# Moving VectorE's softplus steps and an early read by a step in a two-block transformer kernel

## What is computed

```python
def first_block(x, c, ...):
    mod = silu(c) @ w_ada + b_ada                 # 6 x 2048 modulation values
    sh1, sc1, gt1, sh2, sc2, gt2 = split(mod, 6)
    h = rmsnorm(x, g_mix) * (1 + sc1) + sh1
    x = x + (1 + gt1) * mixer(h, ...)             # stick-breaking and sparse attention
    ...

def stick_breaking_attention(q, k, v):            # 8 heads of 128
    z = (q @ k.T) * scale
    log1m = where(past, -softplus(z), 0.0)
    after = cumsum(log1m, reverse=True) - log1m
    w = where(past, exp(log_sigmoid(z) + after), 0.0)
    return w @ v
```

## Time and profile before

| | before |
|---|---|
| median of 3 runs | 2651.7 us (2651.5 to 2653.85) |
| the profiled execution | 2650.92 us |
| its span in the trace | 2649.1 us |
| mean granted clock of TensorE | 0.989 |
| PE busy | 2598.1 us (98%) |
| DVE busy | 1876.9 us (71%) |
| ACT busy | 1236.9 us (47%) |

### The profile page before, as it was taken

The page is one execution under the profiler, slowest core; times in us unless marked ns, Lnnn a source line. Parts: engine busy times, 40 slices in busy tenths (PEclk is TensorE's granted clock), DMA queues, the critical chain, the costliest instruction groups (busy, mean ns, idle before and its releaser), DMA issues. The chain is left out here.

```text
span 2649.1 us, 40816 instructions
## 1 busy us (share of the span) xinstructions
PE 2598.1 (98%) x15329; PEld 2272.6 (86%) x15329; DVE 1876.9 (71%) x2659; ACT 1236.9 (47%) x1625; POOL 129.4 (5%) x203
## 2 busy tenths in 40 slices
PE   7999999999999999999999999999999999999998
PEld 4899888888888888888888888888888888888887
DVE  3468788887888888855666659999776645566554
ACT  3345544445645565544555541115544433444443
POOL 0021122001010000000000000000000000000000
PEclk8999999999999999999999999998999999999999
DMA  9997689768786877755665554554666655666654
GB/s 366 351 303 243 212 263 297 213 200 249 233 265 214 256 244 246 235 190 191 187 186 189 190 158 145 151 151 128 192 189 186 190 189 191 188 187 189 190 183 136
DMA packets 525077, 560.60 MB, mean 212 GB/s; under 512 B 20453, under 2 KB 487841, under 8 KB 524688
## 3 DMA queue, kind: packets, MB, share of 16 engines
q1 hardware_dynamic: 504448, 487.39, 58.3%
q0 software_dynamic: 20496, 71.38, 9.0%
HBM read 553.45 MB, written 2.10 MB: 210 GB/s over the span
## 5 line engine op out<-in xcount | busy, mean ns | idle before, releaser
L1121 DVE TENSOR_TENSOR wlo<-raw,whi 128x1024 fp32r<-128x1024 f32 x794 | 970.4, 1224 | 662.5 <-ACT whi L691 655.8
L691 ACT CAST whi<-raw 128x1024 fp32r<-128x1024 f32 x794 | 830.9, 1050 | 1042.4 <-PE ps L1939 910.9
L1937 PE MATMUL ps<-xhl,whi 128*128 128x512 f32 x3712 | 1172.1, 397 | 6.2 <-DVE wlo L1121 2.8
L1939 PEld LDWEIGHTS ps<-xhl,wlo 128*128 128x128 f32 x3712 | 699.0, 188 | 165.4
L1939 PE MATMUL ps<-xhl,wlo 128*128 128x256 f32 x3712 | 730.9, 278 | 0.0
L1937 PEld LDWEIGHTS ps<-xhl,whi 128*128 128x128 f32 x3712 | 566.8, 189 | 10.2 <-issue 5.6
L1937 PE MATMUL ps<-ghl,whi 128*128 128x512 f32 x1024 | 319.5, 393 | 0.0
L1939 PEld LDWEIGHTS ps<-ghl,wlo 128*128 128x128 f32 x1024 | 192.2, 188 | 44.5
L2297 PE MATMUL ps<-xg,raw 128*128 128x256 f32 x1024 | 221.5, 379 | 0.0
L1937 PE MATMUL ps<-fhl,whi 128*128 128x512 f32 x704 | 219.3, 392 | 0.0
L2297 PEld LDWEIGHTS ps<-xg,raw 128*128 128x128 f32 x1024 | 194.5, 190 | 26.4
(11 more groups left out here) (341 smaller groups left out, 1931.4 us busy)
## 6 DMA issues: line engine op xcount, KB each, us to landing
raw<-in_w_in SPq DMA_DIRECT2D x176, 512.0 KB, 4.9
raw<-in_w_up SPq DMA_DIRECT2D x176, 512.0 KB, 3.6
raw<-in_ffn_w_up SPq DMA_DIRECT2D x128, 512.0 KB, 3.8
raw<-in_ffn_w_down SPq DMA_DIRECT2D x128, 512.0 KB, 3.4
ada<-in_w_ada POOLq DMA_DIRECT2D x109, 512.0 KB, 5.0
raw<-in_w_down SPq DMA_DIRECT2D x88, 512.0 KB, 3.4
att<-in_w_ada SPq DMA_DIRECT2D x32, 1024.0 KB, 11.1
raw<-in_conv_w_pw SPq DMA_DIRECT2D x128, 256.0 KB, 3.3
```

What stands on the lines that cost most here:

```text
L691: nc.scalar.copy(whi[t % SPL][:, :, :], raw[t % RAW][:, :, :]).then_inc(s_hi, 1)
L1121: nc.vector.tensor_tensor(wlo[t % SPL][:, :, :], raw[t % RAW][:, :, :], whi[t % SPL][:, :, :].bitcast(F32), ALU.subtract).then_inc(s_lo, 1)
L1937: mm(o[:, m, :, :], whi[t % SPL][:, c, m * P:(m + 1) * P], x, start=first and c == 0, stop=last and c == KC - 1, skip_group_check=True)
L1939: ins = mm(o[:, m, 0, :], wlo[t % SPL][:, c, m * P:(m + 1) * P], x[:, 0, :], start=False, stop=last and c == KC - 1, skip_group_check=True)
```

## The change

Two places in VectorE's queue change. The read of the first columns of a pair stands behind unit `k = 3`'s split in place of `k = 4`'s. The four softplus steps of head `h` stand in step `25 + 2h` in place of `24 + 2h`: behind split `2s + 5`, two iterations later. The sum (L1387) stays in the even step. The queues of the other engines and all waits are as before.

```diff
@@ -1322,7 +1322,7 @@
                 j, k = t // 10, t % 10
                 c = 4 * (j + 1)
-                if k == 4:
+                if k == 3:
                     read_first(2 * j + 2)
                 if k == 5:
                     read_first(2 * j + 3)
@@ -1385,7 +1385,7 @@
                 if (s - B_STICK) % 2 == 0 and 1 <= h <= HEADS:
                     dve.wait_ge(s_af, h)
                     nc.vector.tensor_tensor(tD[:, :], tD[:, :], bank_f[:, 0:384], ALU.add).then_inc(s_w, 1)
-                if (s - B_STICK) % 2 == 0 and 0 <= h < HEADS:
+                if (s - B_STICK) % 2 == 1 and 0 <= h < HEADS:
 
                     dve.wait_ge(s_soft, h + 1)
                     sv.did(nc.vector.tensor_scalar(tB[:, 0:384], bank_z[:, 0:384], SCALE, 0.0, ALU.mult, ALU.max))
```

## The result

The changed kernel takes 2655.5 us (median of 22 runs, 2652.6 to 2658.3), the kernel before 2652.6 in as many runs of its own (2648.8 to 2655.2). The ratio is 1.0012, with a 95% interval of 1.0006 to 1.0017: +2.9 us, between 1.6 and 4.5. The profiled execution took 2656.2 us, 2654.4 of them span.

The account below looks back on a forecast made before the run. VectorE's waits for ScalarE were taken to hold up TensorE in the stick stage; -2.0 us (read) and +7.0 (later softplus) gave +5.0, between +3.6 and +8.4: 2656.7 us, range 2650.0 to 2660.5.

Parts of the forecast that it names:

- slower: Outcome above the border of 2657.0 us, 0.2% over the kernel before; chance 0.47.
- same: Outcome of no change that a measurement can tell, within about 0.2% (5.3 us); chance 0.41.
- Bound: Stick stage, 215 to 342 us: VectorE's busy time plus its waits sets the length; TensorE idles 6.0 us.
- The new wait of VectorE: Stick heads: the wait moves to the weight split (L1121), 4.67 us in place of 3.46; 6.5 us over all heads.
- TensorE's path: End of stick stage: last suffix sum 8.7 us later from the late softplus; waits of 1.5 to 4 us in nearly every head.
- What comes back: At 372 to 376 us: TensorE's waits of 2.13 and 0.70 us absorb delay, 8.4 - 2.8 = 5.6.
- The transfers' path: Near 372 us: landings released by VectorE's steps come 6.5 to 7.5 us late; the later path decides.
- the +7.0 of the sum: Cost in us at the end of moving the softplus steps one step later, range 5.6 to 8.4.
- The read: First modulation read, 66 to 105 us: waits of 1.63 and 0.35 us go; -2.0 us, range 0 to -2.0.
- The clock rival: Stick stage: TensorE's last new wait lowers its clock, nothing returns at 372 us; +8.1 us, 2659.8 us, chance 0.17.

Follow-up runs that it names:

- soft_by_one: The changed kernel with the softplus steps one iteration later than in the kernel before, instead of a step; 2653.2 us, ratio 1.0005.
- after_notable: The changed kernel with ScalarE's logarithm replaced by a second exponential, so that no table is loaded; 2645.2 us, ratio 0.9973.
- after_spread: The changed kernel with the exchanges of resident weights near 372 us spread over more steps; 2653.8 us, ratio 1.0010.
- before_spread: The kernel before with the exchanges of resident weights near 372 us spread over more steps; 2648.1 us, ratio 0.9987.
- read_only: The kernel before with only the read moved, softplus steps left in the even step; 2647.3 us, ratio 0.9980.
- soft_only: The kernel before with only the softplus steps moved one step later, the read left in place; 2659.3 us, ratio 1.0026.
- log_first_before: The kernel before with only ScalarE's softplus chain put ahead of the exponential that needs VectorE's sum; 2639.0 us, ratio 0.9946.

## Why the prediction was right, by its steps

**How near, and how much of it was luck.** The forecast was +5.0 us, and +2.9 came. That is below the +3.6 at which the sum's own bounds end, and +5.0 is outside the measured interval (1.6 to 4.5). The time of 2655.5 is 1.2 below 2656.7, and not 2.1, only because the kernel before took 2652.6 us in these runs and not the 2651.7 that the forecast was put on. The prediction also gave "slower" (0.47) a little more than "same" (0.41), and it is "same" that came. What it had right is the account of the loss; the gain was sized too small.

**Bound.** Right in the main. Most of what changed is idle time of TensorE, and in the stick stage VectorE's idle time set the length, as soft_by_one and after_notable show.

**The new wait of VectorE.** Right to 0.1 us. The distances between the sums of consecutive heads, after against before, and what was predicted for each:

| head | 1 | 2 | 3 | 4 | 5 | 6 | 7 |
|---|---|---|---|---|---|---|---|
| before, us | 14.97 | 15.82 | 16.35 | 15.30 | 16.23 | 16.35 | 14.70 |
| after, us | 15.04 | 16.44 | 17.54 | 15.91 | 16.84 | 17.57 | 15.91 |
| longer by | 0.07 | 0.62 | 1.19 | 0.61 | 0.61 | 1.22 | 1.21 |
| predicted | 0.1 | 0.6 | 1.21 | 0.6 | 0.6 | 1.21 | 1.21 |

With head 0 (3.6 - 5.53 + 2.85 = +0.9, predicted 1.0) edit 2 costs VectorE 6.5 us, as predicted. What made this possible is that a chain on one engine is a sum of rows: 1.80 us of the row behind the last sum and 2.87 us of the chain gave 4.67, and 4.66 came.

**TensorE's path.** Right in size: +8.7 us predicted for the last suffix sum from edit 2, 8.8 measured (6.0 + 2.8). The waits before the logits (L2117) came in heads 1 to 7, but four of the seven were below the 1.5 us that I had given as the least for nearly all, and one was above the 4 us (0.45, 1.36, 1.58, 3.55, 0.48, 1.36 and 4.53).

**What comes back.** 2.8 us were taken off TensorE's path at 372 us, and +5.6 became +2.7: right. after_spread and before_spread show that this is idle time filled up. The transfers' path, which I let decide and which made 5.6 into 7.0, did not decide in the kernel after: with the transfers spread it stands at 579.6 at the mark, without at 579.8. Edit 2 measured by itself is nevertheless about the +7.0 of the sum: 6.4 us at 577 us on top of the read (579.8 - 573.4) and 7.4 without it, of which 0.6 is that execution's; timed +6.9 alone and 8.2 on top of the read. That the +7.0 fits is in part luck, since the path that it was put on did not decide. The two edits meet in the same idle time near 372 us, so their shares can't be told apart to 1 us.

**The read.** This is the term that was mis-sized: -2.0 was taken, the end of its range. Timed it is -5.3 alone (2.9 to 7.7) and -4.0 beside edit 2 (+2.9 against +6.9). At the last column product it is -2.8 in the profiled executions of before and after, at 577 us -3.7 in that of read_only. Three things were missed.

First, the waits shown are not all that was lost. The first product starts 1.9 us earlier (66.79 to 64.86) where a wait of 1.63 was shown. From the first to the second product of the middle pair 9.03 us pass before and 8.78 after, though the trace of before has no wait there; soft_only shows one of 0.54 us. In the last pair it is 9.30 and 8.78, where 0.35 was shown. Second, the read gains 0.9 us more around 372 us, where TensorE waits less: from the last value product to the mark read_only takes 226.6 us, before 227.5. Third, the wait sometimes costs clock. Four executions had the wait of 1.6 to 1.8 us at 65 us, eight had not. With it the last group of column products started at 145.1, 145.7, 147.0 and 148.1; without it, at 142.4 to 143.0. The latest of the four, log_first_before, had a granted clock of 0.64 from 66 to 70 us, in its table of windows:

```profile
66.00:70.00 4.00, 3.18 (x16) 3.21 (x17) 3.10 (x7) 1.28 (x2) 0.00 (x0) 0.64 0.94 253
```

At this mark the read is thus worth 2.8 to 5.6 us, 3.9 on the average of these executions, and with it the sum would be -3.9 + 7.0 = +3.1. That is reckoned after the fact and from four executions only; how often the kernel before loses clock there isn't shown, and its profiled execution did not. I had weighed the clock against the change, behind new waits, and had not weighed it for the change, behind waits that go.

**The clock rival.** In the stage itself the clock is 0.97 before and after. Behind the wait of 4.53 us it is low. VectorE's head 7 is longer by 1.21 us all the same, just as predicted without the clock, so VectorE's pace wasn't touched, as argued:

```profile
326.00:330.00 4.00, 4.00 (x21) 3.91 (x20) 3.96 (x6) 0.00 (x0) 0.72 (x1) 0.58 0.92 256
```

Open is whether the 3 us near 650 us have more than chance to do with the change.

## What to carry to other kernels

Before moving work behind a wait, look at what the other engine does in its queue between the event and the release: an operation that needs a late result, placed ahead of independent ones, makes all of them late, and here moving the waiting side only renamed the wait. The chain of one head could be summed from rows to 0.1 us, so do this sum for both orders of both engines before choosing. A removed wait of TensorE can be worth more than its length (here 2.0 us shown and 2.8 to 5.6 measured), for the clock behind it is sometimes at the lower level. And look for idle time further down that will hide part of a loss today and not in the next version.

## What the runs showed of the hardware

The same wait of TensorE costs clock in one execution and not in another. At 65 us four executions waited 1.6 to 1.8 us; the granted clock from 66 to 70 us was 1.00, 1.00, 0.76 and 0.64, and the column products then ended up to 3 us apart. In the stick stage before waits 1.84 us and read_only 1.83 us at the same product (L2188), and behind it the clock was 0.65 in one and 1.00 in the other (before first, read_only second, from the tables of windows):

```profile
274.00:278.00 4.00, 3.88 (x22) 3.91 (x23) 3.96 (x5) 0.00 (x0) 0.66 (x1) 0.65 0.75 243
```

```profile
271.00:275.00 4.00, 3.68 (x31) 3.71 (x32) 3.96 (x6) 0.00 (x0) 0.72 (x1) 1.00 0.76 226
```

Near 650 us the kernel before waits 2.23 us and keeps 1.00, and the kernel after waits 1.96 us and has 0.83; read_only waits 2.34 us and has 0.83 too (before first, after second):

```profile
640.00:660.00 20.00, 17.77 (x105) 15.50 (x104) 14.16 (x17) 9.71 (x11) 2.89 (x4) 1.00 0.82 263
```

```profile
640.00:660.00 20.00, 18.04 (x89) 15.68 (x88) 11.37 (x14) 8.09 (x9) 2.17 (x3) 0.83 0.75 236
```

At a clock of 0.83 for 20 us, 20 x 0.17 = 3.4 us of full speed are missing, and the distance between before and after grows by 3.1 us from the mark at 577 to that at 1110. The wait was not longer in the execution of after, whose clock fell to the lower of the two levels (1.2 and 2.4 GHz), than in that of before, whose clock did not. So where a wait of this length stands in a kernel, the marks of a single profiled execution behind it are uncertain by up to about 3 us.
